# Two matrix units run together by token blocks, at the end of the attention projection and of the second feed-forward matrix

## What is computed

```
mixed = (g_ssm * y_ssm + g_att * y_att)
x = x + mixed @ w_o                              # "the projection": 1024 x 1024
h = rms_norm(x, g_norm_mlp)
x = x + square(relu(h @ w_up)) @ w_down          # w_up 1024 x 4096, w_down 4096 x 1024
return rms_norm(x, g_norm_final)
```

## Time and profile before

| | |
|---|---|
| median of 3 runs | 1312.99 us (1312.98 to 1315.13) |
| the profiled execution's own time | 1311.68 us |
| its span, first to last instruction | 1308.4 us |
| PE busy | 1276.9 us, 98% |
| DVE, ACT, POOL busy | 661.9, 528.0, 515.0 us |
| mean granted TensorE clock | 0.997 |
| weights loaded in the part of the change | 512 KB a unit |

### The profile page before, as it was taken

How to read it: one execution, slowest core, us unless ns; L and a number is a source line. 1 busy time by engine, 2 the same in 40 slices (tenths; PEclk the granted TensorE clock), 3 DMA queues, 4 the chain that set the end, 5 groups by cost and what they waited for, 6 DMA issues and landing times.

```text
span 1308.4 us, 19288 instructions
## 1 busy us (share of the span) xinstructions
PE 1276.9 (98%) x6814; PEld 1046.3 (80%) x6814; DVE 661.9 (51%) x1189; ACT 528.0 (40%) x960; POOL 515.0 (39%) x316
## 2 busy tenths in 40 slices
PE   7999999999999999999999999999999999999997
PEld 5887767777788888888888888888778888888886
DVE  5736767676477777787864111111254152250443
ACT  6325456666544544455443222222443232231333
POOL 3332234545332333233224444444334444444442
PEclk9999999999999999999999999999999999999999
DMA  8622310000122222222222333335323332333332
GB/s 239 165 66 48 81 33 2 1 2 2 47 67 81 76 69 64 80 80 64 66 78 81 97 97 97 96 96 176 97 80 98 96 97 96 96 96 96 96 96 96
DMA packets 175746, 107.66 MB, mean 82 GB/s; under 512 B 25074, under 2 KB 163538, under 8 KB 175698
## 3 DMA queue, kind: packets, MB, share of 16 engines
q1 hardware_dynamic: 175458, 106.92, 28.4%
q10 hardware_dynamic: 240, 0.09, 0.0%
HBM read 104.91 MB, written 2.10 MB: 82 GB/s over the span
## 4 chain that ended last, share of the span: by engine, by line
PE 87%; DVE 5%; ACT 4%; issue 3%; POOL 1%; DMA 0%; DVEq 0%; ACTq 0%; SPq 0%; POOLq 0%
PE bank L2191 20%; PE bank L1788 15%; PE bank L2207 11%; PE bank L2197 10%; PE bank L1792 7%; PE bank L2213 5%; PE bank L1928 3%; PE bank L2030 2%; PE bank L1970 2%; PE bank L2009 2%; ACT prob L897 1%; PE bank L1855 1%; PE bank L2171 1%; DVE grp L1583 1%; PE bank L2082 1%
## 5 line engine op out<-in xcount | busy, mean ns | idle before, releaser
L727 POOL TENSOR_TENSOR wlo<-raw,whi 128x1024 fp32r<-128x1024 f32 x181 | 438.2, 2421 | 693.4 <-ACT whi L972 580.2
L972 ACT ACTIVATE whi<-raw 128x1024 fp32r<-128x1024 f32 x158 | 167.6, 1061 | 522.3 <-PE bank L2197 273.4
L1788 PE MATMUL bank<-h_hi,whi 128*128 128x512 f32 x488 | 195.7, 401 | 1.2 <-DVE h_lo L1169 1.2
L1788 PE MATMUL bank<-h_lo,whi 128*128 128x512 f32 x488 | 190.7, 391 | 0.0
L2191 PE MATMUL bank<-h_hi,whi 128*128 128x512 f32 x384 | 150.4, 392 | 1.3 <-DVE grp L1603 0.7
L2191 PE MATMUL bank<-h_lo,whi 128*128 128x512 f32 x384 | 149.7, 390 | 0.0
L1746 DVE TENSOR_TENSOR uf<-rel 128x512 f32<-128x512 f32 x32 | 80.3, 2508 | 90.8 <-ACT rel L1126 90.8
L1792 PE MATMUL bank<-h_hi,wlo 128*128 128x512 f32 x488 | 120.9, 390 | 0.0
L1788 PEld LDWEIGHTS bank<-h_hi,whi 128*128 128x128 f32 x488 | 91.9, 188 | 22.3 <-DVE h_lo L1169 3.0
L747 POOL TENSOR_SCALAR prob<-prob,rsum,gate 128x512 f32<-128x512 f32 (+3 forms) x128 | 76.2, 608 | 84.6 <-DVE rsum L1430 84.5
L1792 PEld LDWEIGHTS bank<-h_hi,wlo 128*128 128x128 f32 x488 | 91.7, 188 | 19.0
(11 more groups left out here) (281 smaller groups left out, 2180.1 us busy)
## 6 DMA issues: line engine op xcount, KB each, us to landing
raw<-in_w_in SPq DMA_DIRECT2D x75, 512.0 KB, 3.8
raw<-in_w_up SPq DMA_DIRECT2D x32, 512.0 KB, 4.0
raw<-in_w_down SPq DMA_DIRECT2D x32, 512.0 KB, 3.7
raw<-in_w_ssm_branch SPq DMA_DIRECT2D x16, 512.0 KB, 3.6
raw<-in_w_in SPq DMA_DIRECT2D x20, 256.0 KB, 3.7
raw<-in_w_attn_branch SPq DMA_DIRECT2D x8, 512.0 KB, 3.6
raw<-in_w_o SPq DMA_DIRECT2D x8, 512.0 KB, 3.7
x_sb<-in_x SPq DMA_DIRECT2D x4, 512.0 KB, 5.9
```

Of the source, the lines that this page charges most:

```text
L727: nc.gpsimd.tensor_tensor(wlo[slot][:], raw[slot][:], whi[slot][:].bitcast(F32), ALU.subtract).then_inc(wlo_ready, units)
L972: nc.scalar.activation(whi[slot][:], raw[slot][:], ACT.Copy).then_inc(whi_ready, 1)
L1788: T.matmul(bank[slot][:], whi[slot][:, k * P:(k + 1) * P], part[:, k, :], start=(k == 0 and n == 0), stop=False)
```

## The change

In half 1 of the projection and of each quarter's `w_down`, units kb = 2 and kb = 3 are no longer run one after the other. A new function, `product_rows_last`, runs them together. It waits for both parts of unit kb = 2 and finishes that unit for the first and the second block (12 matmuls). It then waits for `whi_ready` of unit kb = 3 and does its high matmuls for these two blocks (8), waits for `wlo_ready`, and does its low ones (4), raising `sum_done` for each of the two. Then the third block takes its six matmuls of both units (12), with `sum_done`, and the last block does the same (12). `unit_done` for unit kb = 2 is now raised when the last block has taken its six matmuls out of that unit, that is, after matmul 42 of the 48; before, it was raised after matmul 24. The number of matmuls, their shapes and the counts of all semaphores stay the same. The first halves and units kb = 0 and 1 are as before. No line of ScalarE, DVE, POOL or SyncE changes.

```diff
+            def row_high(slot, to, hi, lo, kb, c): ...   # the former high(c)
+            def row_low(slot, to, hi, kb, c): ...        # the former low(c)
...
+            def product_rows_last(u, banks, hi, lo, order):
+
+                first, second, third, last = order
+                pe.wait_ge(wlo_ready, u + 1)
+                for c in (first, second):
+                    row_high(0, banks[c], hi, lo, 2, c)
+                    row_low(0, banks[c], hi, 2, c)
+                pe.wait_ge(whi_ready, u + 2)
+                for c in (first, second):
+                    row_high(1, banks[c], hi, lo, 3, c)
+                pe.wait_ge(wlo_ready, u + 2)
+                for c in (first, second):
+                    row_low(1, banks[c], hi, 3, c).then_inc(sum_done, 1)
+                for c in (third, last):
+                    row_high(0, banks[c], hi, lo, 2, c)
+                    mm = row_low(0, banks[c], hi, 2, c)
+                    if c == last:
+                        mm.then_inc(unit_done, 1)
+                    row_high(1, banks[c], hi, lo, 3, c)
+                    mm = row_low(1, banks[c], hi, 3, c)
+                    if c == third:
+                        mm.then_inc(sum_done, 1)
+                mm.then_inc(unit_done, 1)
...
-                product_rows(U_WO + j, j % 2, bank[4 * half:4 * half + 4], m_hi, m_lo, kb, WO_ORDER)
+                if half == 0 or kb < 2:
+                    product_rows(U_WO + j, j % 2, bank[4 * half:4 * half + 4], m_hi, m_lo, kb, WO_ORDER)
+                elif kb == 2:
+                    product_rows_last(U_WO + j, bank[4:8], m_hi, m_lo, WO_ORDER)
...
-                    product_rows(q * 16 + (U_MLP + 8 + j), j % 2, bank[4 * (1 - half):4 * (1 - half) + 4],
-                                 u_hi, u_lo, kb, DOWN_ORDER)
+                    if half == 0 or kb < 2:
+                        product_rows(q * 16 + (U_MLP + 8 + j), j % 2, bank[4 * (1 - half):4 * (1 - half) + 4],
+                                     u_hi, u_lo, kb, DOWN_ORDER)
+                    elif kb == 3:
+                        product_rows_last(q * 16 + (U_MLP + 8 + j - 1), bank[0:4], u_hi, u_lo, DOWN_ORDER)
```

More of the change, by code:

```diff
@@ L2199, in product, with row_high, row_low @@
                 mm.then_inc(unit_done, 1)
-            def product_rows(u, slot, banks, hi, lo, kb, order):
[L2204 to L2215, removed]
+            def row_high(slot, to, hi, lo, kb, c):
+                for k in range(2):
+                    for n, part in enumerate((hi, lo)):
+                        T.matmul(to[:], part[:, 2 * kb + k, c * P:(c + 1) * P], whi[slot][:, k * 512:(k + 1) * 512],
+                                 start=(kb == 0 and k == 0 and n == 0), stop=False)
+            def row_low(slot, to, hi, kb, c):
+                for k in range(2):
+                    mm = T.matmul(to[:], hi[:, 2 * kb + k, c * P:(c + 1) * P], wlo[slot][:, k * 512:(k + 1) * 512],
+                                  start=False, stop=(kb == 3 and k == 1))
+                return mm
+            def product_rows(u, slot, banks, hi, lo, kb, order):
                 pe.wait_ge(whi_ready, u + 1)
@@ L2219, in product_rows @@
                     for c in order:
-                        high(c)
+                        row_high(slot, banks[c], hi, lo, kb, c)
                     pe.wait_ge(wlo_ready, u + 1)
                     for c in order:
-                        mm = low(c)
+                        mm = row_low(slot, banks[c], hi, kb, c)
                 else:
```

## The result

The changed kernel takes 1316.12 us (median of 17 runs, 1314.15 to 1317.28), the kernel before 1312.86 us (17 runs). The ratio is 1.0026, with a 95% interval of 1.0019 to 1.0032: 3.4 us slower, 2.5 to 4.2 (the two medians lie 3.3 us apart). The prediction was 1316.6 us.

What follows compares the result with a forecast made beforehand. TensorE, busy 98% of the span, was taken to bound the kernel. The terms 3.6 (projection end) + 0.45 (quarter ends) - 0.4 (kernel end) = 3.65 us, added to 1312.99, gave 1316.6 us, range 1313.3 to 1319.0.

Steps and rivals of the forecast that it cites:

- What bounds the kernel: Whole kernel: TensorE, busy 98% of the span; the chain leaves it behind the projection's last sum and at the end.
- The last sum doesn't move, the others come early: End of projection: block sums move from slots 30, 36, 42, 48 to slots 22, 24, 36, 48.
- TensorE finds its weights: Within each pair of units: weight parts are ready in time, slack 0.5 us, so the waits cost nothing.
- The end of the projection, 3.6 us: ScalarE's later split holds the squares and GpSimd then holds VectorE's scaling: the last square comes 3.6 us later.
- The lower end of the term: End of projection: 2.6 us if GpSimd blocks nothing, with square 3 at 948.75; as a rival, chance 0.13.
- The quarter ends, 0.15 us each: Behind three quarters TensorE waits for the next unit's later split: 0.15 us each, 0.45 us for three.
- The late load behind it: After a quarter end: the next load's split is some 0.7 us late, but hidden by a whole unit.
- The end of the kernel, -0.4 us: End of kernel: earlier sums let the last add start on its signal, a gain of 0.4 us, at least 0.2.
- the larger gain of 1.1: End of kernel: at most 1.1 us gained if the last store also lands in 2.6 instead of 3.3 us.
- The clock: Rival, behind the projection: TensorE's clock falls to 1.2 GHz, costing an estimated 3 us more, 1319.6 us; chance 0.07.
- Sum: Whole kernel: 3.6 + 0.45 - 0.4 = 3.65 us slower, 1316.6 us on the median; chance 0.62.
- the main term: End of projection: squares queued behind ScalarE's later split, plus GpSimd's hold of VectorE; 3.6 us, between 2.6 and 4.2.

Runs made afterwards that it cites:

- split_behind: Changed kernel, but ScalarE splits the first w_up unit behind all four blocks of the projection's second half; ratio to the kernel before 0.9999 (0.9990 to 1.0008).
- pool_later: Changed kernel, but GpSimd makes the first w_up unit's low part only after VectorE has scaled all four projection blocks; ratio to the kernel before 1.0018.
- done_at_36: Changed kernel with unit_done at slot 36, third sum at 42; ratio to before 1.0021. Its _warm variant adds 15 useless matmuls in TensorE's gaps; one run, no ratio.
- proj_only: Changed kernel with the four w_down quarters as before; only the projection's last two units run together; ratio to the kernel before 1.0026 (1.0015 to 1.0036).
- split_between: Changed kernel, but ScalarE splits the first w_up unit between the third and fourth block of the projection's second half; ratio to the kernel before 1.0006.
- both_mended: The split_between kernel with unit_done at slot 36 in the quarters alone; ratio to the kernel before 1.0000 (0.9991 to 1.0009).
- three_mended: The both_mended kernel plus GpSimd's low part of the first w_up unit made only after VectorE's four scalings; ratio to the kernel before 0.9992.
- warm: Changed kernel with 19 useless matmuls in TensorE's three gaps between the projection's turned blocks; ratio to the kernel before 1.0029 (1.0018 to 1.0040).

## Why the prediction was right

- *What bounds the kernel.* One reading was off. The text has the chain leave TensorE behind the projection's last sum. The chain leaves it two blocks earlier, behind the second block's sum (its add starts at 942.27), and from there on runs on ScalarE: a block takes 1.55 us there, and sums come every 1.36. The backlog from this is the 0.4 us that earlier sums can gain, and the forecast's numbers for the end of the kernel use it.
- *The last sum doesn't move, the others come early.* As forecast: adds 0 and 1 ran from 940.61, which is their forecast place of 939.10 and the 1.51 us by which the anchor is later. At the projection this brought nothing, as the squares were held; split_behind shows the 0.41 us that it brings without the hold.
- *TensorE finds its weights.* Right: no wait within the pairs shows in the chain after.
- *The end of the projection, 3.6 us.* Measured 3.48 at the last square (15.49 less 12.01). The split started 9.52 us behind the anchor, forecast 943.63 less 934.11, the same. The scaling of block 0 took 1.54, forecast 1.58. The 0.14 us between 3.62 and 3.48 are there: the scaling was 0.05 us nearer, and add 2 started 0.08 before the row of the scaling ends, where I had put it behind. Of the 3.48 us, 0.97 is GpSimd's hold (pool_later), the rest the queue (split_behind takes all of it back). The lower end of the term holds a slip: square 2 at 947.10 and 1.55 us more give 948.65 and not 948.75, so that without GpSimd's hold the term is 2.5 and not 2.6. pool_later measured 2.51.
- *The quarter ends, 0.15 us each.* Measured 0.16, 0.17 and 0.17 (the places of the units behind the three quarters against the anchor), and done_at_36 removes them. The late load behind it cost nothing, as forecast: ScalarE waited for the load of w_up at 1051.52, TensorE did not.
- *The end of the kernel, -0.4 us.* Measured 0.41. The store's 3.3 us stayed (2.6/2.6/3.3 again), so the larger gain of 1.1 didn't come.
- *The clock.* This is the step that failed, in chance and in size. The forecast gave the fall 7% and leaned on the stretch 177 to 180 in the earlier trace rows, where the clock was 1.00. The same trace has it at 0.50 right behind that stretch, with TensorE busy again, so this row spoke for the fall and not against it:

```profile
180.00:181.00 1.00, 0.74 (x8) 0.61 (x10) 0.08 (x1) 0.60 (x2) 1.00 (x2) 1.00 0.00 0
181.00:182.00 1.00, 1.00 (x14) 1.00 (x14) 0.61 (x1) 0.00 (x0) 1.00 (x1) 0.52 0.06 16
182.00:183.00 1.00, 1.00 (x7) 0.67 (x4) 0.00 (x0) 0.00 (x0) 0.95 (x1) 0.50 0.00 0
```

Behind the projection the clock fell in the profiled run and in all five other kernels in which a queue was held and nothing filled the gaps (proj_only, pool_later, done_at_36, split_between, both_mended). The price was put at 3 us, by counting the 16 matmuls at half pace; it was 0.40, since the clock was back when these started and what ran slowly was the turns. The first w_up matmul came at 957.71, 2.0 us behind its forecast place (954.2 and the anchor's 1.51); most of that took the place of the unit's waits for VectorE's low parts. The sum came out at 4.0 instead of 3.65 us in the trace mainly for this reason.
- *Sum.* 3.48 + 0.40 + 0.50 - 0.41 = 3.97 us, against 378.28 - 374.29 = 3.99 in the traces and 3.4 (2.5 to 4.2) in the runs.
- *What was luck.* The mechanism of the main term was forecast, and the runs confirm it. That the total hit is in part luck: the clock fell after all, and it cost 0.40 us where the forecast's own price for it was 3, which would have given 1319.6, outside the range. The profiled execution's 1315.77 us lies near its forecast of 1315.3 by luck as well: it took 1.9 us around its span and not 3.3, and 1.51 more in front of the anchor. The two differences nearly cancel, and neither comes from the change.

The Trainium skill (SBUF — State Buffer, Who interferes with whom) states that an instruction of VectorE in its two-port mode and one of GpSimd exclude each other for a whole instruction, and counts tensor-scalar among those that can enter this mode, with no word on the kind of scalar. pool_later agrees that a column of SBUF as the scalar doesn't prevent the hold, with 0.48 against 1.54 us for the same operands. The traces don't agree on the length of the hold: the scaling ended 0.28 us after GpSimd, though it takes 0.49 alone. The rule of the Trainium skill (TensorE: Matmul & The Clock Gate, Part 1: The HAM clock gate) is that throttled is the default and activity releases it. I had weighed it against one row, read too short. It agrees with this case's thin stretch: 1.00 with 19 useless matmuls, 0.50 without.

## What to carry to other kernels

When matmuls are regrouped, write down where each semaphore moves, not only where the sums come: a signal that frees a buffer can be worth more than the sum one wanted earlier, as everything in the waiter's queue stands behind it. Then ask which other engine is started at a new moment by that waiter, and what it holds. A gain of earlier sums is bounded by the backlog that was there, here 0.4 us at each of the two ends, and a gain of that size is best read from an anchor in the trace that no edit can reach. When a row of the clock is to speak for a thin stretch, read on past its end.

## What the runs showed of the hardware

- A VectorE tensor-scalar of 128x512, SBUF to SBUF, which started inside a GpSimd tensor-tensor of 128x1024, ended 0.28 us after GpSimd in the trace after, where alone it takes 0.49. So, as far as GpSimd's rows are exact, not all of its own time lay behind GpSimd's end; which part of it runs while it is held, no trace shows. In split_between it took 2.53 us and ended 0.29 us after GpSimd (951.03 and 950.74). A column of SBUF as the scalar doesn't prevent the hold.
- TensorE's clock fell to 1.2 GHz just before 951 us, in the second of two gaps (2.28 and 1.86 us) with four turns of 128 columns between them, and was back at about 957.5; for most of the time between TensorE was busy at half pace. With one gap of 1.60 us in this place it stayed at 1.00 (split_behind, three_mended).
- Whether the clock falls in a thin stretch can differ between executions. The one at 177 to 180 us, in code that all kernels share, was followed by a fall between 178 and 182 in 10 of the 13 traces, both of the kernel before among them, and by none in the others (after, done_at_36_warm, three_mended).
- Matmuls of no use in a free bank kept the clock at 2.4 GHz behind the projection. Their cost is small: the last square came 0.06 us later in warm, 0.03 in done_at_36_warm.
- A slow clock can be nearly free: 0.40 us for over six microseconds at half pace in the trace after, where the next unit would else have waited for VectorE; 0.93 us in done_at_36.
